# The scale and bias of the second block's first layer norm, moved from VectorE to GpSimd

## The chip, the cores and the metric

The kernel runs on one core of one Trainium2 chip. The metric is the time of one execution in microseconds (us) of device time, as the median of several runs. A core has engines with queues of their own: TensorE (PE, matrix products, with PEld for its weight loads), VectorE (DVE), ScalarE (ACT), GpSimd (POOL) and SyncE (SP, which only issues DMAs here). They are held in step by semaphores: an instruction adds to one when it is done, and another engine waits until it has reached a number.

## The reference

Input x is 256 tokens of 1024 features, float32. A first block of two layers (each: feed-forward, a mixer of three kinds, feed-forward) is followed by a second block of one layer, and only that one is touched here:

```python
def hybrid_layer(x, w_in, conv_w, w_pool, pool_scale, w_out, ln1_g, ln1_b,
                 w_up, ffn_conv_w, ffn_conv_b, w_down, ln2_g, ln2_b, rel_bias):
    ...                                                   # attention, convolution, pooling
    mix = jnp.concatenate([attn, conv, pool], axis=-1) @ w_out
    x = layer_norm(DEEPNORM_ALPHA * x + mix, ln1_g, ln1_b)
    up = causal_dwconv(x @ w_up, ffn_conv_w) + ffn_conv_b   # w_up: 1024 x 5632
    u, g = jnp.split(up, 2, axis=-1)
    ff = (u * jax.nn.silu(g)) @ w_down                      # w_down: 2816 x 1024
    return layer_norm(DEEPNORM_ALPHA * x + ff, ln2_g, ln2_b)
```

layer_norm subtracts the row's mean, divides by its deviation, multiplies by g and adds b. Its result is used twice: turned (features on partitions) as the input of x @ w_up, and unturned as the residual that DEEPNORM_ALPHA scales.

## The kernel before

x lies in SBUF as two tiles of 128 tokens (t = 0, 1) by 1024 features. Every product in float32 is made of three passes: each operand is split into a high part (rounded by ACT) and a low part (operand minus high part, by DVE), and high x high, low x high and high x low are added up in PSUM. Weights come in 1 MB tiles of 256 columns or rows by SP's DMAs into six slots; act_high (L455) makes the high part of a tile, dve_low (L460) the low part.

**The first layer norm of the second block** is split. dve_ln(n = 0) and act_ln take x + mix to (x - mean) / deviation in place in x. pe_turn_ln (L816) transposes this into PSUM in eight chunks c of 128 features, and counts the chunks of t = 1 on the semaphore turned. Scale and bias are then put on the turned chunks, where they are one number per partition: even chunks by ACT (L892), odd ones by DVE (L908), both from PSUM into the SBUF tile lin. ACT rounds each to hT's high part (L897), and DVE subtracts for the low part, hT[1] (L913, 128x256, lin and hT[0] both in SBUF). PE's first gate product (L579 for the high weights, L582 for the low ones) takes the chunks in order and waits for each one's low part. The order on DVE is written out in dve_turned_ln: linear of c + 1, low of c, low of c + 1, for c = 0, 2, 4, 6, and behind them the low part of the first up weights (L460), for which PE's second product of group 0 (L598 high, L602 low) waits.

**The unturned x** gets its scale and bias later, from dve_affine: one multiplication (L923) and one addition (L925) of 128x1024 for each t, with ln_gb, the norm's g and b spread over all partitions in SBUF. Nothing needs them before the end of the feed-forward part, where dve_ln(n = 1) adds ALPHA * x to the down product.

**The feed-forward part** runs over 11 groups of 256 hidden features: over_groups calls the group for 0 and 1, a loop for 2 to 9, and 10. PE does gate and up of group g + 1 and then down of group g (L475), so the down product of 10 stands last; it finishes its four halves (t, h) one after the other, and DVE's half_in (L2193, L2194) takes each as it comes. dve_affine runs at the end of DVE's group 1 for t = 0 and of group 10 for t = 1.

**The second layer norm** reuses ln_gb. So SP loads ln2's g and b (load_ln, L1977) only when both affines are done, which it learns from the semaphore lin_dve (L2410). dve_ln(n = 1) waits for the loads ahead of centred(0) (L2205); scaled (L2216) ends the kernel, and ACT stores the result.

**GpSimd** (pool_second) prepares the convolution and the pooling of this layer, from L2351 to L2381. Its last instruction is L2381, and it has no work in the feed-forward part.

Of the kernel before, what the change touches and what calls it, by code (L numbers as in the profile page):

```python
# [18 lines left out]
ALU = mybir.AluOpType  # L19
# [5 lines left out]
NT = SEQ // P  # L25
KC = D // P
# [157 lines left out]
def build(nc, a, out):  # L184
    packed_cols = constants()[1]
    ctx = ExitStack()
    with ctx:
        def sb(name, shape):
            return ctx.enter_context(nc.sbuf_tensor(name, shape, F32))
# [8 lines left out]
        x_in = ctx.enter_context(nc.semaphore("x_in"))  # L198
# [29 lines left out]
        S = {n: ctx.enter_context(nc.semaphore(n)) for n in names}  # L228
        past = dict.fromkeys(names, 0)
# [7 lines left out]
        x = sb("x", [P, NT, D])  # L237
# [111 lines left out]
        ln_gb, o = area(o, 2, D)  # L349
# [116 lines left out]
        def products_done(eng, uses, kind, more=0):  # L466

            eng.wait_ge(used[kind], uses.now(kind, more) + 1)
# [76 lines left out]
        def later(g):  # L545
            return not isinstance(g, int) or g >= 2
# [371 lines left out]
                low(c)  # L918
                low(c + 1)

        def dve_affine(dve, t):
            dve.wait_ge(x_in, 16 * 3)
            dve.tensor_tensor(x[:, t, :], x[:, t, :], ln_gb[:, 0, :], ALU.mult).then_inc(S["lin_dve"], 1)  # L923
            dve.wait_ge(S["lin_dve"], KC // 2 + 2 * t + 1 + past["lin_dve"])
            dve.tensor_tensor(x[:, t, :], x[:, t, :], ln_gb[:, 1, :], ALU.add).then_inc(S["lin_dve"], 1)  # L925

        def pe_tile2(pe, uses, n, part):
            bank = psum[4 + n % 3]
# [1256 lines left out]
        def dve_ln(dve, uses, kind, n, link):  # L2185

            def half_in(t, h):
                if (t, h) != HALVES[-1]:
                    dve.wait_ge(S["half_done"], 3 * n + 2 * t + h + 1 + past["half_done"])
                else:  # L2190
                    products_done(dve, uses, kind, -1)
                xs = x[:, t, h * 512:(h + 1) * 512]
                link(dve.scalar_tensor_tensor(xs, xs, ALPHA, psum[4 + 2 * t + h][:, :], ALU.mult, ALU.add))  # L2193
                ins = dve.bn_stats(lnstat[:, h, :], xs)  # L2194
                if h == 1:
                    link(ins)
                    dve.bn_aggr(lnvar[:, t, :], lnstat).then_inc(S["stats_ready"], 1)
                    dve.wait_ge(S["stats_ready"], STATS[NT * n + t] + past["stats_ready"])

            def inverse_root(t):  # L2200
                dve.wait_ge(S["rms_root"], NT * n + t + 1 + past["rms_root"])
                link(dve.reciprocal(rstd[:, 4 + t:5 + t], rstd[:, t:t + 1]))

            def centred(t):
                link(dve.scalar_tensor_tensor(x[:, t, :], x[:, t, :], lnvar[:, t, 0:1], ln_gb[:, 0, :],  # L2205
                                              ALU.subtract, ALU.mult))

            def flat(t):
                for at in (slice(0, 512), slice(512, D)):
                    dve.tensor_scalar(x[:, t, at], x[:, t, at], lnvar[:, t, 0:1], rstd[:, 4 + t:5 + t],  # L2210
                                      ALU.subtract, ALU.mult).then_inc(S["normed"], 1)

            def scaled(t, parts=1):
                for i in range(parts):
                    at = slice(i * D // parts, (i + 1) * D // parts)
                    dve.scalar_tensor_tensor(x[:, t, at], x[:, t, at], rstd[:, 4 + t:5 + t], ln_gb[:, 1, at],  # L2216
                                             ALU.mult, ALU.add).then_inc(S["normed"], 1)

            half_in(0, 0)
            half_in(0, 1)  # L2220
            half_in(1, 0)
            inverse_root(0)
            if n == 0:
                dve.scalar_tensor_tensor(lnbias[:, 0:1], lnvar[:, 0, 0:1], -1.0, rstd[:, 4:5], ALU.mult, ALU.mult)\
                   .then_inc(S["stats_ready"], 1)
                half_in(1, 1)
                inverse_root(1)
                return flat(1)
            half_in(1, 1)
            dve.wait_ge(x_in, 16 * (1 + 2 * n + 2))  # L2230
            centred(0)
            scaled(0)
            centred(1)
            inverse_root(1)
            scaled(1, 2)

        def dve_second(dve, uses, link):
# [80 lines left out]
            def group(g, par_, more):  # L2318
                if later(g):
                    dve.wait_ge(S["taps_act"], g * 2 - 2 + past["taps_act"])  # L2320
                dve.tensor_scalar(tap_now[:, par_], view[:, :, :, bass.ds(g * 2, 2)], 1.0, None,
                                  ALU.mult).then_inc(S["taps_picked"], 1)
                dve.wait_ge(S["taps_picked"], g + 1 + past["taps_picked"])
                for j in range(2):
                    dve_sum_half(dve, 0, low2, whole2, g, 0, j)
                if not final(g):
                    dve_low(dve, uses, f"gate{1 - par_}", more + par_)
                else:
                    dve_low(dve, uses, f"down{par_}", more, "gate")
                other_taps(g, par_, 0, 1)  # L2330
                for j in range(2):
                    dve_sum_half(dve, 0, low2, whole2, g, 1, j)
                if not final(g):
                    dve_low(dve, uses, f"up{1 - par_}", more + par_)
                other_taps(g, par_, 1, 0)
                dve.wait_ge(S["taps_done"], g * 2 + 2 + past["taps_done"])
                dve.wait_ge(S["silu_done"], g + 1 + past["silu_done"])
                dve_hidden(dve, taps[:, par_, 0, :], par_, g, 0, uses)
                if not final(g):
                    dve_low(dve, uses, f"down{par_}", more, "down")  # L2340
                if isinstance(g, int) and g:
                    dve_affine(dve, int(g > 1))

            over_groups(dve, group)
            uses.ffn("gate")
# [2 lines left out]
        def pool_second(pool, link):  # L2348
            mult, add = ALU.mult, ALU.add
            pool.wait_ge(S["x_updated"], past["x_updated"])  # L2350
            link(pool.memset(wpool, 0.0))  # L2351
            pool.wait_ge(S["proj_ready"], 5 + past["proj_ready"])
            pool.wait_ge(S["params_ready"], 1 + past["params_ready"])

            link(pool.tensor_tensor(cz, proj[:, CC2:CC2 + 2, 1:], proj[:, CX2:CX2 + 2, 1:], mult))
            for c in range(2):
                ins = pool.tensor_scalar(mix[:, 4 + c, :], cz[:, c, :], par2c[:, 4 + c:5 + c], None, mult)
            link(ins)
            part = proj[:, CC2:CC2 + 2, 1:]
            for lag in (1, 2):  # L2360
                for c in range(2):
                    i = 2 * (2 - lag) + c
                    ins = pool.tensor_scalar(part[:, c, lag:], cz[:, c, 0:SEQ - lag], par2c[:, i:i + 1], None, mult)
                link(ins)
                link(pool.tensor_tensor(mix[:, 4:6, lag:], mix[:, 4:6, lag:], part[:, :, lag:], add))
            pool.wait_ge(S["proj_ready"], 9 + past["proj_ready"])
            p_ = proj[:, PI2:PI2 + 2, 1:]
            u, v = pl[:, 0], pl[:, 1]
            link(pool.tensor_copy(u, p_))
            link(pool.tensor_tensor(u[:, :, 1:], u[:, :, 1:], p_[:, :, 0:SEQ - 1], add))  # L2370
            link(pool.tensor_copy(v, u))
            link(pool.tensor_tensor(v[64:P, 0, 2:], v[64:P, 0, 2:], u[64:P, 0, 0:SEQ - 2], add))
            link(pool.tensor_tensor(v[:, 1, 2:], v[:, 1, 2:], u[:, 1, 0:SEQ - 2], add))
            link(pool.tensor_copy(u, v))
            link(pool.tensor_tensor(u[:, 1, 4:], u[:, 1, 4:], v[:, 1, 0:SEQ - 4], add))
            link(pool.tensor_copy(v, u))
            link(pool.tensor_tensor(v[64:P, 1, 8:], v[64:P, 1, 8:], u[64:P, 1, 0:SEQ - 8], add))
            link(pool.tensor_tensor(v, v, const("poolw").rearrange("p (a b) -> p a b", a=2), mult))
            pool.tensor_tensor(u, v, p_, ALU.subtract).then_inc(S["pool_ready"], 1)
            pool.wait_ge(S["proj_ready"], 10 + past["proj_ready"])  # L2380
            pool.tensor_tensor(mix[:, 4:6, :], mix[:, 4:6, :], proj[:, CB2:CB2 + 2, 1:], mult)\  # L2381
                .then_inc(S["mixc_ready"], 1)


        @block.sync
        def _(sp):
# [20 lines left out]
            uses.each(TILE2_SLOTS)  # L2407
            sp_out(sp, uses, 0, a["w_out_2"], OUT2_SLOTS, OUT2_PAIRS)
            sp_ffn(sp, uses, 0, a["w_up_2"], DFF, a["w_up_2"], 0, a["w_down_2"])
            sp.wait_ge(S["lin_dve"], KC // 2 + 2 * NT + past["lin_dve"])  # L2410
            load_ln(sp, "ln2_g_2", "ln2_b_2")

        @block.gpsimd
# [159 lines left out]
```

## Time and profile before

| | |
|---|---|
| three runs | 1401.67, 1405.10, 1405.12 us; median 1405.1 |
| span of the profiled execution | 1403.4 us |
| PE busy | 1360.7 us (97%) |
| PE weight loads busy | 1183.8 us (84%) |
| DVE busy | 965.5 us (69%) |
| ACT busy | 737.1 us (53%) |
| POOL busy | 158.0 us (11%) |
| mean granted clock of TensorE | 0.995 of full speed |

The profile is of one execution; its span reaches from the first to the last instruction, and what a run takes beyond it is the start and the end of the program. A timeline row gives the start in us from the span's start, the duration, the engine, the line in the kernel, the operation, what it writes and reads, and how many instructions were put together (x2); in brackets the idle time before it and who ended it. DVE and ACT rows put together in this way overlap a little. Durations of POOL are rough.

### The profile page before, as it was taken

How to read it: one execution, taken by the hardware profiler on the slowest of the kernel's cores; microseconds unless marked ns; L12 is line 12 of the kernel's file. 1: busy time of each engine (PE TensorE's matmuls, PEld its weight loads, DVE VectorE, ACT ScalarE, POOL GpSimd, SP SyncE). 2: the span in 40 equal slices, each digit the busy share in tenths (PEclk: the TensorE clock that was granted, in tenths of full speed). 3: DMA queues.
4: the chain of work that ended last, by engine and by line, in shares of the span. 5: the costliest groups of instructions: out<-in, count | busy, mean ns of one | idle time of the engine just before them, and what ended most of it. 6: DMA issues, size and time to landing. Idle time of an engine off the chain costs nothing.

```text
span 1403.4 us, 24875 instructions
## 1 busy us (share of the span) xinstructions
PE 1360.7 (97%) x9767; PEld 1183.8 (84%) x9767; DVE 965.5 (69%) x1277; ACT 737.1 (53%) x1036; POOL 158.0 (11%) x155
## 2 busy tenths in 40 slices
PE   8999999998999999999999999999999999999996
PEld 7888889987788888888888988788888898788885
DVE  5666666677776556766656777776565676898788
ACT  6444457464654445644447655464444444765552
POOL 3000000196000000000000059200000033000000
PEclk9999999999999999999999999999999999999998
DMA  9756355210776545755519210275562953465531
GB/s 338 255 180 190 114 184 163 76 47 2 232 255 196 186 143 181 246 196 179 179 66 300 76 62 4 88 264 192 184 202 95 313 167 106 153 205 198 196 103 60
DMA packets 172516, 230.58 MB, mean 164 GB/s; under 512 B 4671, under 2 KB 153847, under 8 KB 172181
## 3 DMA queue, kind: packets, MB, share of 16 engines
q1 hardware_dynamic: 169952, 223.75, 48.9%
q10 hardware_dynamic: 1877, 5.59, 1.1%
q8 instruction: 57, 0.93, 0.3%
q0 software_dynamic: 608, 0.12, 0.0%
q14 instruction: 22, 0.18, 0.0%
HBM read 228.39 MB, written 2.63 MB: 165 GB/s over the span
## 4 chain that ended last, share of the span: by engine, by line
PE 88%; DVE 7%; ACT 2%; issue 1%; POOL 1%; DMA 0%; POOLq 0%; DVEq 0%; ACTq 0%
PE bank L475 36%; PE bank L598 27%; PE bank L602 14%; PE bank L1327 3%; PE bank L579 1%; DVE proj L1803 1%; PE bank L582 1%; PE bank L1013 1%; PE bank L1200 1%; PE bank L1152 1%; DVE work L779 1%; ACT hT L865 0%; DVE down_lo L460 0%; DVE gate_lo L460 0%; PE bank L836 0%
## 5 line engine op out<-in xcount | busy, mean ns | idle before, releaser
L460 DVE TENSOR_TENSOR down_lo<-w_down,down_hi 128x2048 fp32r<-128x2048 f32 x67 | 154.9, 2312 | 98.9 <-ACT down_hi L455 98.9
L598 PE MATMUL bank<-hT,up_hi 128*128 128x512 f32 x880 | 220.4, 392 | 0.0
L662 ACT ACTIVATE work<-bank 128x256 f32<-128x256 f32 x176 | 66.7, 384 | 265.2 <-PE bank L602 255.9
L598 PE MATMUL bank<-hT,gate_hi 128*128 128x512 f32 x800 | 199.1, 391 | 0.0
L460 DVE TENSOR_TENSOR gate_lo<-w_gate,gate_hi 128x2048 fp32r<-128x2048 f32 x67 | 153.9, 2296 | 61.6 <-ACT gate_hi L455 61.5
L455 ACT ACTIVATE down_hi<-w_down 128x2048 fp32r<-128x2048 f32 x67 | 128.6, 1920 | 117.8 <-PE bank L475 116.6
L598 PEld LDWEIGHTS bank<-hT,up_hi 128*128 128x128 f32 x880 | 158.2, 189 | 28.9 <-issue 0.6
L460 DVE TENSOR_TENSOR up_lo<-w_up,up_hi 128x2048 fp32r<-128x2048 f32 x72 | 162.5, 2257 | 21.5 <-ACT up_hi L455 21.5
L598 PEld LDWEIGHTS bank<-hT,gate_hi 128*128 128x128 f32 x800 | 146.7, 188 | 28.2
L475 PE MATMUL bank<-down_hi,ff_hi 128*128 128x512 f32 x400 | 156.2, 391 | 0.0
L475 PE MATMUL bank<-down_lo,ff_hi 128*128 128x512 f32 x400 | 156.2, 391 | 0.0
L475 PE MATMUL bank<-down_hi,ff_lo 128*128 128x512 f32 x400 | 155.6, 389 | 0.0
L668 DVE TENSOR_TENSOR work<-bank,work 128x256 f32<-128x256 f32 x176 | 73.0, 420 | 112.8 <-ACT work L662 112.8
L455 ACT ACTIVATE up_hi<-w_up 128x2048 fp32r<-128x2048 f32 x72 | 136.2, 1892 | 7.5 <-PE bank L475 7.5
L455 ACT ACTIVATE gate_hi<-w_gate 128x2048 fp32r<-128x2048 f32 x67 | 128.2, 1914 | 9.6 <-PE bank L475 5.3
L602 PEld LDWEIGHTS bank<-hT,up_lo 128*128 128x128 f32 x880 | 120.0, 190 | 8.6
L602 PE MATMUL bank<-hT,up_lo 128*128 128x256 f32 x880 | 122.7, 282 | 0.0
L602 PEld LDWEIGHTS bank<-hT,gate_lo 128*128 128x128 f32 x800 | 109.1, 190 | 7.8
L602 PE MATMUL bank<-hT,gate_lo 128*128 128x256 f32 x800 | 111.6, 282 | 0.0
L475 PEld LDWEIGHTS bank<-down_hi,ff_lo 128*128 128x128 f32 x400 | 75.1, 188 | 16.0
L475 PEld LDWEIGHTS bank<-down_hi,ff_hi 128*128 128x128 f32 x400 | 75.3, 188 | 14.3
L1869 POOL TENSOR_TENSOR proj<-proj 128x512 f32<-128x512 f32 x2 | 4.2, 2106 | 734.7 <-ACT proj L1551 734.7
(347 smaller groups left out, 2276.3 us busy)
## 6 DMA issues: line engine op xcount, KB each, us to landing
w_gate<-in_ffn_w_gate_dram SPq DMA_DIRECT2D x44, 1024.0 KB, 5.3
w_up<-in_ffn_w_up_dram SPq DMA_DIRECT2D x44, 1024.0 KB, 5.3
w_down<-in_ffn_w_down_dram SPq DMA_DIRECT2D x44, 1024.0 KB, 5.1
w_up<-in_w_in_dram SPq DMA_DIRECT2D x12, 1024.0 KB, 9.7
w_down<-in_w_in_dram SPq DMA_DIRECT2D x11, 1024.0 KB, 6.3
w_gate<-in_w_up_dram SPq DMA_DIRECT2D x11, 1024.0 KB, 5.1
w_up<-in_w_up_dram SPq DMA_DIRECT2D x11, 1024.0 KB, 5.1
w_down<-in_w_down_dram SPq DMA_DIRECT2D x11, 1024.0 KB, 5.0
```

The costliest lines, as they stand in the source:

```text
L455: act.activation(staged[kind][0][:, 0:cols], slot[sl][:, 0:cols], ACT.Copy).then_inc(high[sl], 1)
L460: dve.tensor_tensor(staged[kind][1][:, 0:cols], slot[sl][:, 0:cols], staged[kind][0][:, 0:cols].bitcast(F32), ALU.subtract).then_inc(split ...
L475: mm = pe.matmul(out_, lhs(l_), rhs(r_), start=first and i == 0, stop=last and i == 2, **kw)
L579: pe.matmul(psum[j][:, :], w[0][:, c, j * P:(j + 1) * P], hpair[:, :, c, :], start=c == 0, stop=False)
L582: mm = pe.matmul(psum[j][:, 0:SEQ], w[1][:, c, j * P:(j + 1) * P], hT[0][:, c, :], start=False, stop=c == KC - 1)
L598: pe.matmul(bank[:, :], w[0][:, c, at], hpair[:, :, c, :], start=c == 0, stop=False)
L602: mm = pe.matmul(bank[:, 0:SEQ], w[1][:, c, at], hT[0][:, c, :], start=False, stop=c == KC - 1)
L662: act.activation(to[:, q, j * SEQ:(j + 1) * SEQ], psum[2 * q + j][:, SEQ:], ACT.Copy)\
L668: dve.tensor_tensor(to[:, q, at], psum[2 * q + j][:, 0:SEQ], from_[:, q, at], ALU.add)\
L779: dve.tensor_scalar(hN[:, t, at], x[:, t, at], rstd[:, 6 + t:7 + t], None, ALU.mult)\
L1013: mm = pe.matmul(bank[:, q_at.start:q_at.start + k_at.stop], q[:, q_at], k[:, k_at], start=True, stop=True)
L1327: mm = pe.matmul(view(bank[at, head(j)]), chain[lhs][at, q, :], view(right), start=True, stop=True)
```

## The change

The affine of both tiles is taken from DVE's groups 1 and 10 and given to POOL, as four instructions in a row at the end of pool_second. POOL waits for the loads of ln1 (x_in) and for all of the norm's transposes (turned at 16, since PE reads x until then). The instructions count on x_updated instead of lin_dve. The two that need both affines wait on that: SP ahead of the loads of ln2, and DVE ahead of the last norm.

```diff
-        def dve_affine(dve, t):
-            dve.wait_ge(x_in, 16 * 3)
-            dve.tensor_tensor(x[:, t, :], x[:, t, :], ln_gb[:, 0, :], ALU.mult).then_inc(S["lin_dve"], 1)
-            dve.wait_ge(S["lin_dve"], KC // 2 + 2 * t + 1 + past["lin_dve"])
-            dve.tensor_tensor(x[:, t, :], x[:, t, :], ln_gb[:, 1, :], ALU.add).then_inc(S["lin_dve"], 1)
+        def pool_affine(pool):
+            pool.wait_ge(x_in, 16 * 3)
+            pool.wait_ge(S["turned"], 2 * KC + past["turned"])
+            for t in range(NT):
+                pool.tensor_tensor(x[:, t, :], x[:, t, :], ln_gb[:, 0, :], ALU.mult).then_inc(S["x_updated"], 1)
+                pool.wait_ge(S["x_updated"], 2 * t + 1 + past["x_updated"])
+                pool.tensor_tensor(x[:, t, :], x[:, t, :], ln_gb[:, 1, :], ALU.add).then_inc(S["x_updated"], 1)
+                pool.wait_ge(S["x_updated"], 2 * t + 2 + past["x_updated"])
...
+            if n == 1:
+                dve.wait_ge(S["x_updated"], 2 * NT + past["x_updated"])
             half_in(0, 0)
...
-                if isinstance(g, int) and g:
-                    dve_affine(dve, int(g > 1))
...
             pool.tensor_tensor(mix[:, 4:6, :], mix[:, 4:6, :], proj[:, CB2:CB2 + 2, 1:], mult)\
                 .then_inc(S["mixc_ready"], 1)
+            pool_affine(pool)
...
-            sp.wait_ge(S["lin_dve"], KC // 2 + 2 * NT + past["lin_dve"])
+            sp.wait_ge(S["x_updated"], 2 * NT + past["x_updated"])
             load_ln(sp, "ln2_g_2", "ln2_b_2")
```

## Rows read from the trace of the kernel before

**Rows 1.** The page, part 4: shares of the chain that ended last, by engine.

```profile
PE 88%; DVE 7%; ACT 2%; issue 1%; POOL 1%; DMA 0%; POOLq 0%; DVEq 0%; ACTq 0%
```

**Rows 2.** The chain in order of time, 1204 to 1404: start, us, what.

```profile
1208.64 0.70 PE bank L579 x2
...
1374.17 0.97 PE bank L602 x8
...
1386.91 1.15 DVE x L923
...
1388.08 1.23 DVE x L925
```

**Rows 3.** The timeline of the end, 1370 to 1404: start, us, engine, line, operation.

```profile
1388.23 0.40 PE L475 MATMUL bank<-gate_hi,ff_lo 128*128 128x512 f32 x1
...
1389.22 0.68 DVE L2193 SCALAR_TENSOR_TENSOR x<-x,bank 128x512 f32<-128x512 f32 x1
...
1392.32 0.39 PE L475 MATMUL bank<-gate_hi,ff_lo 128*128 128x512 f32 x1
...
1393.74 0.69 DVE L2193 SCALAR_TENSOR_TENSOR x<-x,bank 128x512 f32<-128x512 f32 x1
```

**Rows 4.** The timeline of the turning stage, 1198 to 1240.

```profile
1206.65 1.33 PE L816 MATMUL bank<-cst,x 128*128 128x128 f32 x8 [0.32 <-DVE x L2210]
...
1208.07 0.76 DVE L913 TENSOR_TENSOR hT<-work,hT 128x256 fp32r<-128x256 f32 x2 [0.39 <-ACT hT L897]
...
1210.67 0.90 DVE L913 TENSOR_TENSOR hT<-work,hT 128x256 fp32r<-128x256 f32 x2
...
1211.50 0.62 PE L579 MATMUL bank<-hT,gate_hi 128*128 128x512 f32 x2
...
1212.85 2.29 DVE L460 TENSOR_TENSOR up_lo<-w_up,up_hi 128x2048 fp32r<-128x2048 f32 x1
...
1214.29 1.99 PE L598 MATMUL bank<-hT,up_hi 128*128 128x512 f32 x8
...
1216.11 1.11 PE L602 MATMUL bank<-hT,up_lo 128*128 128x256 f32 x8
```

**Rows 5.** DMA issues of the end, 1380 to 1404: KB, us from issue to landing.

```profile
work<-in_ln_b_dram SPq DMA_DIRECT2D x1, 512.0 KB, 4.8
```

**Rows 6.** The timeline of SP's queue, the last two weight fills.

```profile
1341.67 16.99 SPq L485 DMA_DIRECT2D w_down<-in_w_down_dram  x2
```

**Rows 7.** Groups of POOL's instructions by line and form: busy us, mean ns.

```profile
L1878 POOL TENSOR_TENSOR proj<-proj,par 128x512 f32<-128x512 f32 x2 | 2.1, 1040 | 0.2
...
L1889 POOL TENSOR_TENSOR proj<-proj,par 128x456 f32<-128x456 f32 x2 | 1.9, 946 | 0.2
...
L2355 POOL TENSOR_TENSOR proj<-proj 128x512 f32<-128x512 f32 x1 | 1.1, 1096 | 36.2 <-DVE proj L949 36.2
...
L2375 POOL TENSOR_TENSOR work<-work 128x252 f32<-128x252 f32 x1 | 0.7, 716 | 0.1
```

**Rows 8.** The timelines of DVE and of POOL around 1172.

```profile
1171.51 2.72 DVE L460 TENSOR_TENSOR gate_lo<-w_gate,gate_hi 128x2048 fp32r<-128x2048 f32 x1
...
1171.32 0.76 POOL L2372 TENSOR_TENSOR work<-work 64x254 f32<-64x254 f32 x1
...
1172.16 2.57 POOL L2373 TENSOR_TENSOR work<-work 128x254 f32<-128x254 f32 x1
```

**Rows 9.** The timelines of DVE and of POOL around 876, in the first block.

```profile
875.48 2.32 DVE L1803 SCALAR_TENSOR_TENSOR proj<-proj,par 128x249 f32<-128x249 f32 x2
...
876.40 1.12 POOL L1891 TENSOR_TENSOR mix<-mix,proj 128x456 f32<-128x456 f32 x1
```

**Rows 10.** The timelines of DVE and of POOL around 1147.

```profile
1147.48 0.69 DVE L949 TENSOR_SCALAR proj<-bank 128x512 f32<-128x512 f32 x1 [2.05 <-PE bank L475]
...
1146.33 1.86 POOL L2363 TENSOR_SCALAR proj<-proj,work 128x255 f32<-128x255 f32 x2
```

**Rows 11.** Busy us (and counts) by window: PE, PEld, DVE, ACT, POOL, PEclk, DMA.

```profile
1396.00:1400.00 4.00, 0.00 (x0) 0.00 (x0) 3.90 (x5) 0.00 (x0) 0.00 (x0) 0.53 0.28 113
```

## The prediction, made before the changed kernel was run

> **What bounds the kernel now.** I read the page first: of the chain that ended last TensorE (PE) carries 88% and VectorE (DVE) 7% [rows 1]. So work taken off DVE is worth nothing by itself. It counts only where PE is waiting for DVE, or where the end of the kernel is DVE's own work. The chain of waits says where that is in the second block's feed-forward part [rows 2]. From the first gate product (L579, 1208.64) to the last gate/up product (L602, ended 1375.14) every piece of the chain is a PE piece, one behind the other. One of the two groups that lose their affine, group 1, lies in there. At 1386.91 the chain enters L923 and L925, the affine of t = 1 in group 10, and stays on DVE to the end.
>
> Then the timelines of two stretches. At the end [rows 3], PE's first finished half of the last down product is done at 1388.23 + 0.40 = 1388.63, but DVE takes it up (L2193) only at 1389.22, since L925 runs from 1388.08 for 1.23 us [rows 2]. In the turning stage [rows 4], where the change puts GpSimd (POOL) to work, PE eats one chunk c per 0.70 us (c = 4 at 1211.50, the up product behind c = 7 at 1214.29, a fourth of the difference). Each chunk waits for one small DVE subtraction (L913, the low part of hT). Those are made just in time: the pair for c = 4 and 5 starts at 1210.67, and c = 4 is used at 1211.50.
>
> **The change part by part.**
>
> *Removed from DVE, group 1* (t = 0): the same two instructions as in group 10, about 2.4 us. PE runs there without a gap [rows 2] and its products hide them: 0 us. If DVE ever fell behind PE there, they would be worth up to 2.4.
>
> *Removed from DVE, group 10* (t = 1): 1.15 + 1.23 us on the chain [rows 2]. What is late next is PE's first half, done at 1388.63. So the tail starts 1389.22 - 1388.63 = 0.59 us earlier, less the 0.03 that a release takes: 0.56. It must not run into a later half: PE's last product is done at 1392.32 + 0.39 = 1392.71, and DVE takes it at 1393.74 - 0.56 = 1393.18, still behind it [rows 3]. All of it reaches the end: -0.6 us.
>
> *The loads of the second norm's scale and bias* (SP, L1977) could go only behind L925, ended 1389.31; the longer takes 4.8 us to land [rows 5], so 1394.5. Their first reader stands behind the sum of 1393.74 and its statistics, and did not wait long, if at all. Now SP's wait is met early, and they go out right behind the last weight fill, near 1359 [rows 6]. Nothing stands behind them on SP's queue: 0 us. DVE's new wait ahead of the last norm asks for POOL work finished some 170 us before: 0 us. Behind it stand only the norm's own steps.
>
> *Added on POOL*: four TENSOR_TENSOR of 128x1024 with both inputs in SBUF, in a row, from the last transpose on (PE L816, done at 1206.65 + 1.33 = 1207.98 [rows 4]). I take 1208.1 for the start. The trace has no such operation of this size. The nearest rows: 512 elements take 1.04 and 1.10 us, 456 take 0.95, 252 take 0.72 [rows 7]. (1.040 - 0.946) / 56 = 1.68 ns an element gives 1.04 + 512 x 1.68 = 1.90 us. From 252 to 512 elements it is (1.096 - 0.716) / 260 = 1.46 ns, so 1.84. Twice 1.10 is 2.19. I take 1.95, close to the first, whose rows are nearest in size, with 1.84 and 2.19 as ends. Four of them are 8 us, to about 1216.4, and lie over DVE's eight subtractions.
>
> *What POOL does to DVE meanwhile* decides. DVE's L460 takes 2.29 us alone [rows 4]. At 1171.51 it took 2.72, beginning inside a POOL operation (1171.32 + 0.76), and the next POOL operation (L2373, 254 elements) took 2.57 where 252 elements otherwise took 0.72: it ended 0.5 us after DVE's [rows 7, 8]. So the two exclude each other for a whole operation. With many in a row they alternate one for one: DVE's two L1803 at 875.48 took 2.32 us together, and between them POOL ran a whole operation (876.40) in 1.12 us, hardly stretched [rows 9]. L460's delay of 0.43 puts the moment of release at 1171.94, 0.14 before POOL's recorded end; the gap to the next POOL operation is 0.08 [rows 8]. A subtraction of L913's size (a pair takes 0.76 [rows 4]) just about fills these. One POOL operation, the gap and about 0.03 make a cycle of 1.95 + 0.08 + 0.03 = 2.06 us, and one DVE subtraction gets through per cycle. What reads only PSUM, as L908 does, is not held: L949 kept its 0.69 us at 1147.48 while two POOL operations ran from 1146.33 for 1.86 us [rows 10].
>
> The schedule by hand: low 0 goes at 1208.07 as now. POOL's first operation waits for it and ends at about 1210.25. Low 1 goes at 1210.12, low 2 at 1212.18, low 3 at 1214.24, low 4 at 1216.30, done at 1216.68. By then POOL's four are through, and low 5 to 7 follow without a wait. PE takes c = 4 at 1216.73, not at 1211.50: +5.2 us. From c = 5 on it keeps its old pace. The next thing due from DVE, up_lo (L460, 2.29 us), would end near 1220.7, and PE wants it at 1216.11 + 5.2 = 1221.3 [rows 4]: 0.6 us spare. Since PE is the chain without a gap from there to 1375 [rows 2], nothing gives the 5.2 back.
>
> Bounds of that term. If POOL starts ahead of low 0, every low is one cycle later in the order: 5.8. If it starts 0.3 us later, low 1 slips by as well: 4.9. With 1.84 us an operation take off 4 x 0.11, with 2.19 add 4 x 0.24: outer ends 4.5 and 6.8. Less than nothing is excluded, since POOL takes no work off this stretch.
>
> The Trainium skill, "GPSIMD Engine Reference", section 4.1, says to leave two-input elementwise work to VectorE, GpSimd being about twice as slow. An estimate by that, 2 x 1.2 = 2.4 us an operation, would add 4 x 0.45 = 1.8 us to the delay; the rows of 512 elements speak for less, and my sum keeps 1.95. The same skill, "SBUF — State Buffer", section "Who interferes with whom", has the rule that speaks against this change: a VectorE instruction with two SBUF inputs and a GpSimd one that reads SBUF block each other fully, in order of issue. The trace agrees (2.72 for 2.29, 2.57 for 0.72).
>
> **Sum.** +5.2 - 0.6 = +4.6 us on a span of 1403.4, so 1408.0. The median of the three runs is 1405.1, 1.7 us above the profiled span, and the change touches nothing outside the span. Forecast 1405.1 + 4.6 = 1409.7; with the bounds (4.5 - 0.6 and 6.8 - 0.6) 1409.0 to 1411.3.
>
> **The rivals.**
>
> *A: DVE is not held (not slower).* If DVE's short subtractions pass ahead of a waiting POOL operation each time, only POOL is stretched, and its first user is 170 us away. The point that decides is whether two DVE operations in a row go through one gap; the 249-element ones at 875.48 did not [rows 9], which speaks against it. Result -0.6: 1404.5. If pairs pass but not more, half of the holds remain and up_lo takes one of them: +1 to +4, 1405.5 to 1408.5.
>
> *B: the clock falls too.* PE would do 0.7 us of work per 2.06 us for 8 us, where now it is busy throughout. After PE's last product (1392.71) the granted clock was 0.53 on the mean of 1396 to 1400 [rows 11], that is at 1.2 GHz for most of it, after nothing but idleness. What a third of busy time does, no row shows. If it falls near the end of the stage, a further 4 to 8 us run at 1.2 GHz and lose up to half of that: +2 to +4, 1411.7 to 1413.7.
>
> *C: the change does less than it says.* POOL would have to start after low 7, some 4.5 us late. POOL has nothing else to do then, so little speaks for it. It would hold L460 and its successors instead, where the spare is below 1 us: near 1406.
>
> **How the numbers follow.** Forecast case 0.62; A 0.13 (0.08 whole, 0.05 part); B 0.18; C and others 0.07. A measurement of this kernel can tell about 0.3%, 4.2 us, from no change. My +4.6 lies close above that, and the three runs of before lie 3.4 us apart (1401.67 to 1405.12), so of the forecast case I put two thirds above the bound; B is above it nearly whole. Slower: 0.41 + 0.17 + 0.02 = 0.60. Faster needs more than -4.2, which no case gives; 0.04 for medians that fall on different ones of those levels. Same: 0.36. The range goes from 1405.0 (A in part, C) to 1413.0 (most of B).
>
> **What would show it.** Right: the eight L913 spread over about 10 us, four of them near 2 us long; four POOL rows of about 2 us from 1208 to 1216.5; the first up product (L598, now 1214.29) near 1219.5, and all of PE behind it as much later; L2193 right behind PE's first half; the ln2 loads near 1364. Wrong: L913 pairs of 0.76 to 0.92 as now (A); a granted clock below 1.00 between 1210 and 1225 (B); POOL operations outside 1.8 to 2.2 us.

## The result: slower by 9.4 us between the profiles, twice what was forecast

| | before | changed |
|---|---|---|
| runs | 1401.67, 1405.10, 1405.12, 1405.32 us | 1414.29, 1414.57, 1423.89, 1423.99 us |
| median | 1405.1 us | 1419.2 us; ratio 1.010, interval 1.008 to 1.013 |
| both again, later | 1405.1 us (31 runs) | 1413.9 us (10 runs); ratio 1.008, interval 1.005 to 1.011 |
| span of the profiled execution | 1403.4 us | 1412.8 us |
| POOL busy | 158.0 us | 168.5 us |
| mean granted clock of TensorE | 0.995 | 0.990 |

The forecast was 1409.7 us in a range of 1405.0 to 1413.0, so the time lies above the range. Some executions take some 10 us more, 8 of 105 of the kernel before and 6 of 14 of the changed one; without them the changed kernel's first runs stand at 1414.4 us, still above the range, and the reading below explains the 9.4 us between the two profiled spans.

First the shares of the chain that ended last, in the page of the changed kernel, and some of its pieces in order of time (start us, us, what):

```profile
PE 87%; DVE 8%; ACT 2%; issue 1%; POOL 1%; DMA 0%; DVEq 0%; ACTq 0%; POOLq 0%
```

```profile
1207.95 2.93 DVE hT L913 x2
...
1211.33 4.55 DVE hT L913 x2
...
1216.33 2.07 DVE hT L913
1218.45 1.22 PE bank L579 x2
...
1384.07 0.97 PE bank L602 x8
...
1398.63 0.70 DVE x L2196
```

Against [rows 2]: where the chain had PE's gate product from 1208.64 on, it now lies on DVE's subtractions until 1218.45. The two affine pieces at 1386.91 and 1388.08 are gone, and DVE's first sum of the last norm (L2196 here, L2193 before) stands in their place.

The timeline of the turning stage, to be laid beside [rows 4]:

```profile
1206.54 1.33 PE L816 MATMUL bank<-cst,x 128*128 128x128 f32 x8 [0.32 <-DVE x L2213]
...
1207.95 2.93 DVE L913 TENSOR_TENSOR hT<-work,hT 128x256 fp32r<-128x256 f32 x2 [0.39 <-ACT hT L897]
1208.01 2.58 POOL L925 TENSOR_TENSOR x<-x,work 128x1024 f32<-128x1024 f32 x1 [26.45 <-PE bank L816]
...
1210.67 2.42 POOL L927 TENSOR_TENSOR x<-x,work 128x1024 f32<-128x1024 f32 x1
...
1211.26 4.62 DVE L913 TENSOR_TENSOR hT<-work,hT 128x256 fp32r<-128x256 f32 x2
...
1213.18 2.42 POOL L925 TENSOR_TENSOR x<-x,work 128x1024 f32<-128x1024 f32 x1
...
1215.68 2.43 POOL L927 TENSOR_TENSOR x<-x,work 128x1024 f32<-128x1024 f32 x1
...
1218.45 1.22 PE L579 MATMUL bank<-hT,gate_hi 128*128 128x512 f32 x2 [0.86 <-DVE hT L913]
...
1223.73 2.43 PE L598 MATMUL bank<-hT,up_hi 128*128 128x512 f32 x8
...
1226.00 1.11 PE L602 MATMUL bank<-hT,up_lo 128*128 128x256 f32 x8
```

The pair of subtractions that took 0.76 us takes 2.93, and the next pair takes 4.62 instead of 0.92. POOL's four instructions run one behind the other, 2.50 us from start to start, and one subtraction gets through in each. And PE's rows have changed length: the chunk c = 4 takes 1.22 us where it took 0.62, the up product 2.43 where it took 1.99. Why is in the busy time by windows (us of PE, PEld, DVE, ACT, POOL with counts, then the granted clock):

```profile
1208.00:1212.00 4.00, 2.01 (x7) 1.56 (x8) 4.00 (x4) 1.73 (x5) 3.91 (x2) 0.87 0.00 0
1212.00:1216.00 4.00, 2.30 (x8) 1.52 (x6) 4.00 (x3) 0.66 (x2) 3.84 (x3) 0.50 0.00 0
1216.00:1220.00 4.00, 3.13 (x9) 2.45 (x10) 3.85 (x6) 1.70 (x4) 2.11 (x1) 0.50 0.00 0
1220.00:1224.00 4.00, 4.00 (x14) 3.42 (x14) 2.38 (x3) 0.24 (x1) 0.00 (x0) 0.50 0.07 15
1224.00:1228.00 4.00, 4.00 (x21) 3.36 (x21) 2.50 (x3) 3.54 (x6) 0.00 (x0) 0.92 1.04 370
```

TensorE falls to 1.2 GHz (a granted clock of 0.50) about 3 us after the last transpose and is back at 2.4 GHz only in the last window, though its last wait for DVE ended at 1218.45.

So the 9.4 us are three terms. The last transpose is done at 1206.54 + 1.33 = 1207.87, 0.11 before its old 1207.98, and all times are taken from there.

- The hold: c = 4 starts at 1218.45, before at 1211.50 - 0.11 = 1211.39: **+7.06**.
- The clock: the up product's low part (L602) starts at 1226.00, before at 1216.11 - 0.11 = 1216.00, which is +10.0; what is beyond the hold is **+2.9**. From there to the last gate/up product both kernels take the same: 1384.07 - 1226.00 = 158.07 and 1374.17 - 1216.11 = 158.06.
- The tail: from 1384.07 to the span's end 28.73 us, before 1403.4 - 1374.17 = 29.23: **-0.5**.

The end of the kernel, in the timeline [rows 3]:

```profile
1398.12 0.39 PE L475 MATMUL bank<-gate_hi,ff_lo 128*128 128x512 f32 x1
...
1398.63 0.69 DVE L2196 SCALAR_TENSOR_TENSOR x<-x,bank 128x512 f32<-128x512 f32 x1 [1.82 <-PE bank L475]
```

DVE now waits for PE's first half (done at 1398.51); before, the finished half waited for DVE. SP issued the loads of ln2 at 1368.61 and 1369.12, landed in 5.8 and 6.5 us, long before their reader.

### The profile page after: what moved, and what is told of

The parts are those of the page before. It is cut to its first block, busy times and chain, and to the rows that moved or that the text cites. A ratio compares the mean times of both kernels' runs of the same rounds, so it can differ in the third digit from the quotient of the medians.

```text
span 1412.8 us, 24878 instructions
## 1 busy us (share of the span) xinstructions
PE 1368.0 (97%) x9767; PEld 1188.7 (84%) x9767; DVE 968.5 (69%) x1273; ACT 737.5 (52%) x1036; POOL 168.5 (12%) x159
## 4 chain that ended last, share of the span: by engine, by line
PE 87%; DVE 8%; ACT 2%; issue 1%; POOL 1%; DMA 0%; DVEq 0%; ACTq 0%; POOLq 0%
PE bank L475 35%; PE bank L598 27%; PE bank L602 14%; PE bank L1330 3%; PE bank L579 1%; DVE proj L1806 1%; DVE hT L913 1%; PE bank L582 1%; PE bank L1016 1%; PE bank L1203 1%; PE bank L1155 1%; DVE work L779 0%; DVE down_lo L460 0%; DVE gate_lo L460 0%; PE bank L836 0%
## 5 line engine op out<-in xcount | busy, mean ns | idle before, releaser
L460 DVE TENSOR_TENSOR down_lo<-w_down,down_hi 128x2048 fp32r<-128x2048 f32 x67 | 154.9, 2312 | 98.9 <-ACT down_hi L455 98.9
L460 DVE TENSOR_TENSOR gate_lo<-w_gate,gate_hi 128x2048 fp32r<-128x2048 f32 x67 | 153.8, 2296 | 63.1 <-ACT gate_hi L455 63.1
L460 DVE TENSOR_TENSOR up_lo<-w_up,up_hi 128x2048 fp32r<-128x2048 f32 x72 | 162.5, 2257 | 22.7 <-ACT up_hi L455 22.7
L668 DVE TENSOR_TENSOR work<-bank,work 128x256 f32<-128x256 f32 x176 | 73.0, 420 | 112.9 <-ACT work L662 112.9
L602 PEld LDWEIGHTS bank<-hT,up_lo 128*128 128x128 f32 x880 | 120.1, 190 | 8.6
L602 PE MATMUL bank<-hT,up_lo 128*128 128x256 f32 x880 | 122.7, 282 | 0.0
L602 PEld LDWEIGHTS bank<-hT,gate_lo 128*128 128x128 f32 x800 | 109.1, 190 | 7.8
L602 PE MATMUL bank<-hT,gate_lo 128*128 128x256 f32 x800 | 111.6, 282 | 0.0
```

Of the source, the lines that this page charges most:

```text
L460: dve.tensor_tensor(staged[kind][1][:, 0:cols], slot[sl][:, 0:cols], staged[kind][0][:, 0:cols].bitcast(F32), ALU.subtract).then_inc(split ...
L602: mm = pe.matmul(bank[:, 0:SEQ], w[1][:, c, at], hT[0][:, c, :], start=False, stop=c == KC - 1)
L668: dve.tensor_tensor(to[:, q, at], psum[2 * q + j][:, 0:SEQ], from_[:, q, at], ALU.add)\
```

## The experiments

Theory H: a POOL instruction with SBUF inputs and a DVE subtraction exclude each other, one subtraction passes for each POOL instruction, and PE, which has no slack, is late by all of it. Theory K: TensorE, left without work in between, loses its clock besides, and that is a term of its own. Rival W: the loss comes from the edit's other side (the new waits on x_updated, the loads that go early, the instructions gone from DVE), and the stretched subtractions only come along. For every kernel the same length is read: from the end of the last transpose to the start of the last gate/up product, 166.19 us before and 176.20 after the change, and the tail behind it. Since it starts at the transposes, what happens earlier in an execution doesn't enter.

### Is it GpSimd's presence alone?

The first kernel is the one before, unchanged, with four multiplications on POOL that nobody needs, of the same size and in the same place, each chained to the one ahead. The line left out of the cut only views proj, a tile of the mixer, as one long row, flat.

```diff
                 .then_inc(S["mixc_ready"], 1)
+            pool.wait_ge(S["turned"], 2 * KC + past["turned"])
...
+            for i in range(4):
+                link(pool.tensor_tensor(flat[:, 0:D], flat[:, D:2 * D], cst[:, 0:D], mult))
```

> The kernel before, with the affine left on VectorE, and beside it four GpSimd operations that nobody needs, at the very place of the change: tensor_tensor of 128x1024 with both inputs in SBUF. Theory T (GpSimd's reads shut out VectorE's two-input subtractions, and the clock falls because TensorE starves): all of the loss without the gain of the tail, so the changed kernel plus 0.5: span near 1413.4, time near 1415, the first up product near 1223.7, clock 0.50 from 1212 to 1224. Rival R1 (the loss comes from the new waits on x or from what the change takes off VectorE): as before, span 1403.4, time 1405.

Its timeline:

```profile
1208.06 2.94 DVE L913 TENSOR_TENSOR hT<-work,hT 128x256 fp32r<-128x256 f32 x2 [0.39 <-ACT hT L897]
1208.06 10.16 POOL L2386 TENSOR_TENSOR proj<-proj,cst 128x1024 f32<-128x1024 f32 x4 [26.35 <-PE bank L816]
```

The up product starts at 1223.84. The length is 176.19 us, +10.0, equal to the changed kernel's within 0.01; median 1414.6 (10 runs), ratio 1.007 (1.004 to 1.010). The tail keeps its 29.23. So the whole loss is made by POOL's instructions, with DVE's work, waits and loads as they were: W falls. The gain of 0.5 in the tail belongs to the removal.

The second has three fills in their place, which read nothing.

```diff
+            for i in range(3):
+                link(pool.memset(flat[:, 0:4 * D], 0.0))
```

> The same place, but three memsets of 128x4096, which write SBUF and read nothing, some 3 us each. T in the narrow form (only GpSimd's reads stand against a second SBUF input of VectorE): L913 pairs stay at 0.76 to 0.92 us, span 1403.4, time 1405. Rival R2 (any GpSimd work on SBUF shuts VectorE out): L913 held 2 to 3 us each, clock falls, span 1411 or more.

```profile
1208.07 10.71 POOL L2386 MEMSET proj<- 128x4096 f32 x3 [26.34 <-PE bank L816]
1208.09 0.76 DVE L913 TENSOR_TENSOR hT<-work,hT 128x256 fp32r<-128x256 f32 x2 [0.39 <-ACT hT L897]
```

POOL is as busy, for 10.71 us, and the pair takes its old 0.76, the next ones 0.92, 0.90 and 0.89. The length is 166.18, the median 1405.2, ratio 0.999 (0.996 to 1.001). Here a busy POOL that only writes does no harm, and one that reads SBUF does.

The third copies, with one input:

```diff
+            for i in range(4):
+                link(pool.tensor_copy(flat[:, 0:2 * D], flat[:, 2 * D:4 * D]))
```

> The kernel before with four GpSimd copies of 128x2048 from SBUF to SBUF at the place of the change: one input, not two, and 2.2 to 2.4 us each by twice the slope of the trace's copies of 512 elements. T: it is reading SBUF at all that shuts out VectorE's second input, so the subtractions are held for a copy each, as with two inputs: first up product 8 to 9.5 us later, clock down, span 1412 to 1414. Rival (only a two-input GpSimd operation does it): as with the memsets, span 1403.4.

```profile
1207.94 7.98 POOL L2386 COPY proj<-proj 128x2048 f32<-128x2048 f32 x4 [26.30 <-PE bank L816]
1207.95 4.19 DVE L913 TENSOR_TENSOR hT<-work,hT 128x256 fp32r<-128x256 f32 x2 [0.39 <-ACT hT L897]
1210.25 0.70 PE L579 MATMUL bank<-hT,gate_hi 128*128 128x512 f32 x2 [2.38 <-DVE hT L913]
```

One input is enough. Here POOL was 0.01 us ahead, and the subtractions 0 to 3 were held instead of 1 to 4: even the first one waited for a whole copy (1.89 to 1.97 us each), and PE was late from its first chunk on. Four holds remain four, so the lead of a hundredth costs one subtraction more behind the row and not one more hold; it is the order behind the prediction's bound of 5.8 against 5.2. The length is 172.91, +6.7; ratio 1.007 (1.005 to 1.009). The up product was expected 8 to 9.5 us late and came 6.7 late, since a copy took less than the 2.2 to 2.4 us assumed.

### Is the clock a term of its own?

The changed kernel again, with PE given three products that nobody needs ahead of each of the chunks 1 to 4. They fit into the time in which it waits, so the hold stays and only the idleness goes.

```diff
                         for c in range(KC):
+                            if not gained and c in (1, 2, 3, 4):
+                                pe.wait_ge(S["lin_dve"], 1 + past["lin_dve"])
+                                for _ in range(3):
+                                    pe.matmul(psum[3][:, 0:SEQ], ident, cst[:, 0:SEQ], start=True, stop=True)
                             h_ready(pe, n_norm, c, gained)
```

> The changed kernel, with three idle TensorE products of 256 columns ahead of each of the chunks 1 to 4 of the first gate product, so that TensorE has work while VectorE is held. T with two separate parts, hold 7.1 us and clock 2.9 us: the granted clock stays at 1.00 from 1208 to 1228, the hold stays, span near 1410, time near 1411.5. Rival R3 (the clock falls for another reason, or the hold follows from the slow clock): clock 0.50 again, span 1413 or more.

The timeline, in which the program's lines are four further on, and the windows:

```profile
1206.23 1.46 PE L580 MATMUL bank<-cst 128*128 128x256 f32 x6
...
1207.87 0.73 PE L583 MATMUL bank<-hT,gate_hi 128*128 128x512 f32 x2 [0.18 <-DVE hT L917]
...
1218.27 2.00 PE L602 MATMUL bank<-hT,up_hi 128*128 128x512 f32 x8
```

```profile
1208.00:1212.00 4.00, 3.75 (x18) 3.00 (x19) 4.00 (x3) 1.29 (x3) 3.92 (x2) 1.00 0.00 0
1212.00:1216.00 4.00, 3.52 (x16) 2.41 (x16) 4.00 (x5) 1.29 (x3) 2.96 (x2) 1.00 0.00 0
```

DVE is held as before, each of PE's remaining waits still ends on DVE, but the clock stays at 2.4 GHz, and the up product takes 2.00. The length is 173.37, +7.2, where the changed kernel has +10.0: hold 7.2, clock 2.8. Median 1412.0, ratio 1.004 (1.001 to 1.006). K holds beside H, since nothing but PE's idleness was taken away.

The changed kernel as it is was run once more.

> The changed kernel once more. Of its first four executions two took 1414.3 and 1414.6 us and two 1423.9 and 1424.0, while the kernel before also shows a few executions some 10 us longer. If the 9.5 us more have nothing to do with the change, most executions lie at 1414.5 and a small part at 1424, as with the kernel before; if the change makes them likelier, about half do.

The length is 175.00, +8.8. POOL and DVE alternate in the same 2.50 us, but TensorE stays at 2.4 GHz for 7 us after the last transpose instead of 3, and returns 4 us into the steady part:

```profile
1220.00:1224.00 4.00, 1.11 (x6) 0.67 (x4) 4.00 (x3) 1.29 (x3) 3.84 (x3) 1.00 0.00 0
1224.00:1228.00 4.00, 2.33 (x8) 1.84 (x8) 4.00 (x4) 0.91 (x3) 3.92 (x2) 0.74 0.00 0
1228.00:1232.00 4.00, 3.15 (x11) 2.48 (x10) 3.85 (x6) 0.80 (x2) 0.80 (x1) 0.50 0.00 0
```

So the hold is the same in both profiled executions (c = 4 starts 10.58 and 10.57 us after the last transpose) and the clock's term is not: 2.9 there, 8.8 - 7.1 = 1.7 here.

### How it grows with the dose

Half of it: POOL does t = 0 alone, and DVE keeps t = 1 in group 10 (the waits, left out here, follow suit).

```diff
-            for t in range(NT):
+            for t in (0,):
                 pool.tensor_tensor(x[:, t, :], x[:, t, :], ln_gb[:, 0, :], ALU.mult).then_inc(S["x_updated"], 1)
...
+                if isinstance(g, int) and g > 1:
+                    dve_affine(dve, 1)
...
```

> Half of the change: GpSimd does only the affine of t = 0 at the same place (two operations), VectorE keeps that of t = 1 in group 10. Theory T (each GpSimd operation of 2.42 us holds one subtraction, cycle 2.5 us; clock apart): low 1 and low 2 are held, the chunk c = 2 starts 3.4 us late, nothing of the tail is gained; if the clock stays, span near 1406.9; if it falls as in the whole change, 2 to 3 us more, 1409 to 1410. Rival (the loss isn't proportional to the holds): as the whole change, 1412 or more.

```profile
1213.07 1.22 PE L579 MATMUL bank<-hT,gate_hi 128*128 128x512 f32 x2 [1.54 <-DVE hT L913]
```

The chunk c = 2 comes 5.57 us after the last transpose (1207.50) instead of 2.13, which is the hold, 3.4 for two instructions and 7.06 for four. The length is 171.12, +4.9, so the clock adds 1.5. Median 1410.6, ratio 1.004 (1.001 to 1.006).

All of it, but in small pieces: each of the four instructions is cut into eight of 128 columns.

```diff
-                pool.tensor_tensor(x[:, t, :], x[:, t, :], ln_gb[:, 0, :], ALU.mult).then_inc(S["x_updated"], 1)
-                pool.wait_ge(S["x_updated"], 2 * t + 1 + past["x_updated"])
-                pool.tensor_tensor(x[:, t, :], x[:, t, :], ln_gb[:, 1, :], ALU.add).then_inc(S["x_updated"], 1)
+                for n, op in enumerate((ALU.mult, ALU.add)):
+                    for i in range(8):
+                        at = slice(i * D // 8, (i + 1) * D // 8)
+                        ins = pool.tensor_tensor(x[:, t, at], x[:, t, at], ln_gb[:, n, at], op)
+                    ins.then_inc(S["x_updated"], 1)
+                    if n == 0:
+                        pool.wait_ge(S["x_updated"], 2 * t + 1 + past["x_updated"])
```

> The changed kernel with each GpSimd operation cut into eight of 128x128, at the same place. T: a held subtraction waits for a piece of some 0.5 us instead of 2.4, a cycle of 0.6 us is below TensorE's pace of 0.70 a chunk, so the delay falls from 7 to at most 1 us, the clock stays at 1.00, the tail's gain stays: span 1403 to 1405. Rival (it is GpSimd's total time at this place that counts, some 16 us with the pieces' fixed costs): 1412 or more.

```profile
1207.39 1.02 DVE L913 TENSOR_TENSOR hT<-work,hT 128x256 fp32r<-128x256 f32 x2 [0.39 <-ACT hT L897]
1207.46 28.05 POOL L928 TENSOR_TENSOR x<-x,work 128x128 f32<-128x128 f32 x32 [26.42 <-PE bank L816]
...
1214.03 1.99 PE L598 MATMUL bank<-hT,up_hi 128*128 128x512 f32 x8
...
1232.00 0.47 PE L475 MATMUL bank<-down_hi,ff_hi 128*128 128x512 f32 x1 [1.07 <-DVE down_lo L460]
```

A pair takes 1.02 to 1.25 us, the granted clock stays 1.00, and the up product starts 6.72 us after the last transpose (1207.31) against 6.31. But POOL is at it for 28 us, and DVE's other low parts, each a little longer, end in PE's 1.07 of waiting at 1232. The length is 167.89, +1.7 instead of +10.0; median 1404.7, ratio 1.000 (0.998 to 1.002). At most 1 us had been expected. Beside this stage it is the length of one instruction that decides, not the work.

### How it depends on the place

Three kernels leave the change as it is and make POOL begin later: behind the last subtraction, in the middle of the saturated part in a row, and there one instruction in each of four groups.

```diff
             pool.wait_ge(S["turned"], 2 * KC + past["turned"])
+            pool.wait_ge(S["h_low"], 4 + KC + past["h_low"])
```

> The changed kernel, with GpSimd's four operations begun only when all eight low parts of hT are made. T: the chunks come at their old times and the clock stays, but the row now stands over up_lo, gate_lo and the work of groups 0 and 1, where in group 4 four in a row reached TensorE by at most 0.1 us; here VectorE has no lead yet (up_lo is made 0.97 us before it is wanted), so 1 to 4 us are lost: span 1404 to 1407. Rival (any place but that of the chunks is free): 1402.9.

```profile
1218.10 3.90 DVE L460 TENSOR_TENSOR gate_lo<-w_gate,gate_hi 128x2048 fp32r<-128x2048 f32 x1
...
1222.05 3.68 PE L598 MATMUL bank<-hT,gate_hi 128*128 128x512 f32 x8 [2.05 <-DVE gate_lo L460]
...
1230.87 2.11 PE L598 MATMUL bank<-hT,up_hi 128*128 128x512 f32 x8 [1.40 <-DVE up_lo L460]
```

The subtractions are free here (0.89 to 0.92 a pair) and the up product is in time at 1214.26, but DVE has no lead yet: L460 takes 3.90 instead of 2.29 and PE waits for it, 2.05 and then 1.40 us. TensorE's clock fell as well (0.76 and 0.81 in the windows from 1220 to 1228). The length is 172.04, +5.9, more than the 1 to 4 us expected; median 1411.0, ratio 1.003 (1.001 to 1.006). This is also the place of the prediction's rival C, which priced it near 1406, too low.

```diff
+            pool.wait_ge(S["ff_ready"], 4 + past["ff_ready"])
```

> The changed kernel with GpSimd's four operations in a row, but begun only when hidden group 3 is ready, in the saturated part. One operation by itself cost nothing there (each stretched to 4.3 us by a 2.3 us subtraction). T: four in a row hold VectorE about 7 us within one group, whose spare is some 2.5 us and whatever lead it has: 1 to 4 us lost, clock 1.00, span 1404 to 1407. Rival (in the saturated part nothing reaches TensorE): 1402.9.

```profile
1270.94 4.29 POOL L926 TENSOR_TENSOR x<-x,work 128x1024 f32<-128x1024 f32 x1 [91.38 <-DVE ff_lo L714]
...
1276.07 3.79 DVE L460 TENSOR_TENSOR gate_lo<-w_gate,gate_hi 128x2048 fp32r<-128x2048 f32 x1
...
1279.79 6.08 DVE L2317 SCALAR_TENSOR_TENSOR work<-mix,work 128x255 f32<-128x255 f32 x4
```

Here the same four instructions hold DVE just as hard: four operations that take 1.79 us take 6.08. No PE row waits for any of it. The length is 166.21, 0.0; a loss of 1 us or more had been expected. The holds of these rows come to some 8 us (a TENSOR_SCALAR of 0.17 us took 2.38 as well), and 60 us into the feed-forward part DVE was far enough ahead to take them. Median 1404.1, ratio 0.999 (0.997 to 1.001).

```diff
+                pool.wait_ge(S["ff_ready"], 4 * t + 2 + past["ff_ready"])
                 pool.tensor_tensor(x[:, t, :], x[:, t, :], ln_gb[:, 0, :], ALU.mult).then_inc(S["x_updated"], 1)
                 pool.wait_ge(S["x_updated"], 2 * t + 1 + past["x_updated"])
+                pool.wait_ge(S["ff_ready"], 4 * t + 4 + past["ff_ready"])
```

> The changed kernel, with GpSimd's four operations spread over the feed-forward part: each waits for another hidden group (2, 4, 6, 8) to be ready. T: each holds one VectorE instruction up to 2.4 us, where VectorE has about 2.5 us of idle time in a group of 16.6 us and TensorE is saturated; nothing reaches TensorE, the clock stays at 1.00, and the tail's 0.5 us are gained: span near 1402.9, time near 1404.5. Rival (no spare there): 1 to 2.4 us lost for each, 1408 to 1414.

The length is 166.19, 0.0, the tail 28.75. (Its span of 1401.1 is 2.3 below that of before; 1.8 of it lie ahead of the stage, whose transposes were done at 1206.16 and not at 1207.98, as executions of one kernel differ too.) The ratio was 0.998 (0.996 to 1.000), which looked like a gain, so it was run again:

> GpSimd's four operations one per group, once more with more executions: the tail's 0.5 us are gained and nothing is lost, ratio to the kernel before 0.9996; the rival is the 0.9979 of the first look, which would need a gain of 3 us that no row of its trace shows.

The second time 1.000 (0.998 to 1.002), with the same length (166.18). The 0.5 us of the tail is in the profile; the runs can't tell it.

Last, no GpSimd at all: the kernel before, with both tiles' affines on DVE in group 1.

```diff
-                if isinstance(g, int) and g:
-                    dve_affine(dve, int(g > 1))
+                if isinstance(g, int) and g == 1:
+                    for t in range(NT):
+                        dve_affine(dve, t)
```

> The kernel before, with both affines on VectorE at the end of its group 1, none on GpSimd: four instructions of 1.2 us, 4.9 us together. It tells what the tail is worth by itself. T: VectorE has the spare, the tail starts 0.5 us earlier, span 1402.9. Rival (4.9 us in one group are more than its spare): 1 to 2 us lost to TensorE in group 2, 1404 to 1405.

```profile
1241.97 1.22 DVE L923 TENSOR_TENSOR x<-x,work 128x1024 f32<-128x1024 f32 x1
```

Four such instructions, and the length stays 166.19, the tail is 28.73, ratio 1.001 (0.998 to 1.004). All that the change could gain comes from taking the affine of t = 1 out of group 10. GpSimd isn't needed for it. No version is measurably faster than the kernel before.

## Why the prediction failed

**Right.** The views were read rightly as to what bounds the kernel: the loss stands on PE's chain undiminished for 160 us (158.07 against 158.06 behind the stage). The hold goes as the schedule by hand had it: low 0 passes, one subtraction per POOL instruction, no hold behind low 4, chunks 5 to 7 at once. The tail gave 0.5 for a forecast 0.6. Group 1's affine, the new waits and the loads were costed at nothing, and the kernel with POOL's work added and none of these changes has the same loss as the changed one to 0.01 us. Rival A (DVE passes ahead) fell at the first pair of 2.93 us, rival C with POOL's start at 1208.01. Slower by more than 0.3% had the largest chance, 0.60.

**The first step that failed is the price of POOL's instruction.** The sum took 1.95 us with bounds of 1.84 and 2.19; it took 2.42. The cycle became 2.50 instead of 2.06 us, four times 0.44 is 1.8, and 5.2 + 1.8 = 7.0 is the 7.06 that was measured. The bounds came from a line through rows of 252 to 512 elements [rows 7], continued to twice the size, and from twice 1.10. Those rows are the cheap ones. The same view of the kernel before (busy us, mean ns) has others of this size, with two inputs:

```profile
L1893 POOL TENSOR_TENSOR mix<-mix,proj 128x512 f32<-128x512 f32 x2 | 2.5, 1270 | 0.8 <-DVE proj L1803 0.8
...
L2365 POOL TENSOR_TENSOR mix<-mix,proj 128x508 f32<-128x508 f32 x1 | 1.3, 1283 | 0.1
```

They weren't held: beside L2365 (from 1153.81 on) DVE only reads PSUM, and L1893 (from 338.23 on) was ahead of DVE's next instruction with two SBUF inputs.

Twice 1.28 is 2.56, so an upper end taken from these would have covered 2.42, and "twice 1.10" wasn't an upper bound. The Trainium skill, "GPSIMD Engine Reference", section 4.1, with its factor of two against VectorE, had it right: DVE does this same operation in 1.22 us, and 2.42 is 1.98 times that. The prediction set the cheaper of its rows above it.

**The second is the clock.** Rival B had the right size (+2 to +4; measured 2.9 and 1.7) but only 0.18 of the chance, as a case beside the forecast and not as a term of it, with the words that no row shows what a third of busy time does. The trace of before had two rows that come near, both in the first block. At 332 and at 876 PE is busy for 2.40 of 4 us. Behind the first the clock stays at 1.00; some 8 us behind the second, when PE has no gap left, it runs at 1.2 GHz (windows of the kernel before):

```profile
332.00:336.00 4.00, 2.40 (x33) 1.57 (x29) 3.88 (x7) 1.29 (x3) 3.77 (x4) 1.00 0.00 0
...
876.00:880.00 4.00, 2.40 (x56) 1.89 (x48) 3.92 (x6) 1.67 (x3) 3.76 (x4) 1.00 0.02 4
...
888.00:892.00 4.00, 4.00 (x15) 3.41 (x15) 1.43 (x5) 2.07 (x2) 0.00 (x0) 0.50 0.00 0
```

That the gaps of 876 brought that fall is a reading of the rows and not shown by a run. But with one fall behind two such stretches, and with the forecast's own stretch emptier than both (0.70 us of work in each 2.06, for 8 us), the clock was worth more than a chance of 0.18. The kernel with PE filled shows that the idleness makes this term and that it adds to the hold: 7.2 without it, 10.0 with it. With both steps mended the sum is 7.0 + 2.9 - 0.6 = 9.3 on 1403.4; the span came out at 1412.8. Had only the price of the hold been off, the time would have been 1411.5, inside the range; had only the clock been missing, 1412.6, inside too. Both together give 1414.4, and the first runs without the long executions stand there.

**What the range left out.** Each of its ends came from one unknown alone. The price of POOL's instruction and the clock can both go wrong, and in the same direction, since a longer hold starves PE more.

**Open.** In the median of the first four runs another 5 us stand, since two of them took 1424. In the profile of the repeated run, one of that length, they are lost before the change has done anything. Its last transpose is 10.7 us later than in the first profile, and both parts of that lie in the first block: some 2 us by 237 us, behind a fall of the clock from 216 to 228, and most of the rest where TensorE runs at 1.2 GHz between 340 and 356 us, 860 us ahead of the changed place, where the kernel before has 1.00:

```profile
344.00:348.00 4.00, 4.00 (x44) 3.43 (x36) 0.00 (x0) 0.49 (x1) 0.00 (x0) 0.50 0.00 0
```

Such executions occur with the kernel before too, less often (counts above). Among the kernels that keep the change and differ from it only in when or how POOL's row or PE's filling runs (eighths, behind the lows, in group 4, one per group twice, filled), they are 1 of 62, so moving the affine to GpSimd doesn't bring them by itself. What made them 6 of 14 in the changed kernel stays open.

## What to carry to other kernels

Before elementwise work goes from VectorE to GpSimd, look at what VectorE does with SBUF inputs in the same stretch and whether TensorE takes it just in time: in these rows each GpSimd instruction that reads SBUF lets one VectorE instruction with SBUF inputs through, whatever that one's length (0.17 us or 2.29), so short operations on the path suffer most. If it must be GpSimd, put it where VectorE has a lead (60 us into the feed-forward part it cost nothing, 5 us behind the last transpose 5.9 us) or cut it into small pieces (10.0 became 1.7); better, ask first whether another place on VectorE does the same, as it did here. Take the price of a GpSimd instruction from all rows of its kind, the dear ones too. And when a stall on TensorE is forecast, its clock belongs to the sum, with a price and a chance taken from starved stretches elsewhere in the same trace.

## What the runs showed of the hardware that was not expected

- GpSimd's time has a spread at one size. A two-input instruction of 128x1024 took 2.40 to 2.46 us wherever it followed another without being held, 1.20 to 1.23 for each 512 elements; unheld ones of 508 to 512 elements took between 1.04 us [rows 7] and 1.28 us. What sets the spread is open, so these rows don't tell whether the time is in proportion to the size.
- It is the reading of SBUF that holds VectorE. Three fills of 128x4096 over 10.71 us left the pairs of subtractions at 0.76 to 0.92; copies with one input held one subtraction each for their 1.9 us. The Trainium skill, "SBUF — State Buffer", section "Who interferes with whom", says so: a VectorE instruction with two SBUF inputs contends with a GpSimd one that reads SBUF, not with one that only writes it. The fills and the copies agree. A VectorE TENSOR_TENSOR with one of its two inputs in PSUM (L668) wasn't held: a pair kept its 0.76 us at 1275.40 in the kernel with the row in group 4, while POOL ran its second instruction.
- The smallest instructions are held as long as the large ones. A TENSOR_SCALAR of 128x16 with one input in SBUF, 0.17 us alone, took 2.38 beside one POOL instruction (the kernel with one per group):

```profile
1240.00 4.29 POOL L926 TENSOR_TENSOR x<-x,work 128x1024 f32<-128x1024 f32 x1 [60.10 <-DVE ff_lo L714]
1241.95 2.38 DVE L2328 TENSOR_SCALAR work<-work 128x16 f32 x1
```

  In the same rows POOL's own 4.29 us are, as an estimate, 2.4 of work behind a wait for DVE's L460, which ended at 1242.02.
- In the same starved stretch the clock fell 3.1 us after the last transpose in one execution and 7.4 us in another, and it came back some 6 and 4 us after PE's last wait for DVE; so the loss is 2.9 or 1.7 us, with nothing changed in the program.
